# Loading each expert's up matrix in two halves, and waiting for each half in the up pass

## The reference

```python
aff = sigmoid(xt @ w_router)                      # 64 experts, 8 of them per token
...
def expert_block(args):
    rows, e = args
    xb = x_pad[rows]
    h = jax.nn.silu(xb @ w_gate[e]) * (xb @ w_up[e])
    return h @ w_down[e]
...
return (routed + shared).reshape(B, S, D)         # routed: gated sum over the chosen experts
```

## Time and profile before

| | before |
|---|---|
| median of 3 runs | 1285.56 us (1285.19 to 1286.29) |
| the profiled execution's own time | 1285.14 us |
| its span, first to last instruction | 1282.9 us |
| TensorE matmul busy | 1215.6 us (95%) |
| VectorE / ScalarE busy | 366.9 us (29%) / 293.0 us (23%) |
| moved by DMA | 446.60 MB in 70800 packets, mean 348 GB/s |
| queue of SP, share of the 16 engines over the span | 83.9% |

### The profile page before, as it was taken

The page is one execution under the profiler, slowest core; times in us unless marked ns, Lnnn a source line. Parts: engine busy times, 40 slices in busy tenths (PEclk is TensorE's granted clock), DMA queues, the critical chain, the costliest instruction groups (busy, mean ns, idle before and its releaser), DMA issues.

```text
span 1282.9 us, 20916 instructions
## 1 busy us (share of the span) xinstructions
PE 1215.6 (95%) x7984; PEld 768.6 (60%) x7986; DVE 366.9 (29%) x913; ACT 293.0 (23%) x703; POOL 49.8 (4%) x97
## 2 busy tenths in 40 slices
PE   7999999999999999999899989999999999999994
PEld 6775756565565656565677647565656655565652
DVE  0334712221222222221424447222212222222214
ACT  1453312121221212121123313121212212121211
POOL 1331000000000000000012100000000000000000
PEclk9999999999999999999999989999999999999998
DMA  9532499999999999999930525999999999999993
GB/s 345 189 138 122 202 398 421 420 421 423 422 421 422 422 422 421 422 422 421 406 129 1 202 90 214 399 420 421 421 421 421 422 422 421 422 422 422 422 420 130
DMA packets 70800, 446.60 MB, mean 348 GB/s; under 512 B 6880, under 2 KB 10336, under 8 KB 20576
## 3 DMA queue, kind: packets, MB, share of 16 engines
q1 hardware_dynamic: 69744, 442.79, 83.9%
q10 hardware_dynamic: 1008, 3.15, 0.6%
HBM read 444.86 MB, written 1.05 MB: 348 GB/s over the span
## 4 chain that ended last, share of the span: by engine, by line
issue 49%; PE 36%; DMA 10%; DVE 1%; POOL 1%; ACT 1%; SPq 0%; another core or an unknown queue 0%; POOLq 0%; DVEq 0%; ACTq 0%
DMA ring<-in_w_up 10%; PE bank L953 7%; PE bank L978 6%; PE bank L946 6%; PE bank L524 4%; PE bank L987 3%; PE bank L582 3%; PE bank L543 2%; POOL soft L501 1%; PE bank L846 1%; DMA ring<-in_w_in_a 1%; PE bank L960 1%; PE bank L758 1%; PE bank L864 1%; PE bank L558 1%
## 5 line engine op out<-in xcount | busy, mean ns | idle before, releaser
L953 PE MATMUL bank<-ring,work 128*64 128x256 f32 x2048 | 232.9, 380 | 21.3 <-DMA ring<-in_w_up 21.3
L978 PE MATMUL bank<-ring,work 128*64 128x512 f32 x1024 | 233.8, 598 | 4.3 <-ACT work L1057 4.3
L946 PE MATMUL bank<-ring,work 128*64 128x256 f32 x2048 | 232.4, 379 | 2.3 <-DMA ring<-in_w_gate 1.3
L946 PEld LDWEIGHTS bank<-ring,work 128*64 128x64 f32 x2048 | 150.9, 137 | 100.4 <-issue 39.8
L953 PEld LDWEIGHTS bank<-ring,work 128*64 128x64 f32 x2048 | 154.4, 137 | 91.9 <-issue 29.0
L1554 DVE TENSOR_TENSOR yhalf<-bank,yhalf 128x512 fp32r<-128x512 f32 x128 | 88.6, 692 | 239.4 <-ACT yhalf L1057 239.4
L987 PE MATMUL bank<-yhalf,back 128*128 128x512 f32 x512 | 150.8, 417 | 2.8 <-DVE yhalf L1554 2.8
L978 PEld LDWEIGHTS bank<-ring,work 128*64 128x64 f32 x1024 | 68.1, 136 | 134.3 <-issue 128.4
L1546 DVE SCALAR_TENSOR_TENSOR work<-work,gcol,bank 128x256 f32<-128x256 f32 x64 | 30.8, 481 | 370.2 <-issue 289.7
L1057 ACT ACTIVATE yhalf<-bank 128x512 fp32r<-128x512 f32 x128 | 76.5, 598 | 220.5 <-PE bank L978 220.5
L987 PEld LDWEIGHTS bank<-yhalf,back 128*128 128x128 f32 x512 | 87.3, 190 | 39.7 <-issue 23.8
(11 more groups left out here) (149 smaller groups left out, 754.5 us busy)
## 6 DMA issues: line engine op xcount, KB each, us to landing
ring<-in_w_gate SPq DMA_DIRECT2D x128, 1024.0 KB, 19.5
ring<-in_w_up SPq DMA_DIRECT2D x128, 1024.0 KB, 21.2
ring<-in_w_down SPq DMA_DIRECT2D x128, 1024.0 KB, 18.9
ring<-in_w_in_b SPq DMA_DIRECT2D x3, 3072.0 KB, 23.4
ring<-in_w_out SPq DMA_DIRECT2D x4, 2048.0 KB, 8.2
ring<-in_w_mem_kv SPq DMA_DIRECT2D x2, 2048.0 KB, 18.6
ring<-in_w_in_a SPq DMA_DIRECT2D x1, 3072.0 KB, 17.4
ring<-in_w_shared_gate SPq DMA_DIRECT2D x2, 1024.0 KB, 6.0
```

The costliest lines, as they stand in the source:

```text
L946: last = pe.matmul(gate_bank[slots_of(e), 0:HID], xg[:, k, slots_of(2 * j + e)], w[e][:, k, 0, :], start=(k == 0), stop=(k == KT - 1))
L953: last = pe.matmul(up_bank[slots_of(e), 0:HID], xg[:, k, slots_of(2 * j + e)], w[e][:, k, 1, :], start=(k == 0), stop=(k == KT - 1))
L978: last = pe.matmul(yb[half][slots_of(e), :], hT[:, f, slots_of(e)], w[e][:, f, half * 512:half * 512 + 512], start=(f == 0), stop=(f == FT ...
```

## The change

Each expert now has four parts instead of three: gate, first half of up (row blocks 0 to 3), second half of up (row blocks 4 to 7), down. Each half has a semaphore of its own (`up_first_landed`, `up_second_landed`). In `reload` both experts' first halves are issued ahead of both second halves. In the up pass PE waits for both first halves ahead of k = 0, and for both second halves ahead of k = 4. The bytes moved are the same, and so is the arithmetic.

```diff
-                dst, src = expert_loads(ring[:, slot, :], *srcs)[part]
-                sp.dma_start(dst, src).then_inc(sem(("gate_landed", "up_landed", "down_landed")[part] + f"{k}_{l}"), 16)
+                gate_up_down = expert_loads(ring[:, slot, :], *srcs)
+                if part in (1, 2):
+                    dst, src = gate_up_down[1]
+                    rows = slice((part - 1) * KT // 2, part * KT // 2)
+                    sp.dma_start(dst[:, rows, :], src[:, rows, :]).then_inc(sem(("up_first_landed", "up_second_landed")[part - 1] + f"{k}_{l}"), 16)
+                else:
+                    dst, src = gate_up_down[2 * part // 3]
+                    sp.dma_start(dst, src).then_inc(sem(("gate_landed" if part == 0 else "down_landed") + f"{k}_{l}"), 16)
...
                 sp.wait_ge(sem(f"hidden_{l}"), units)
-                for k in (2 * b, 2 * b + 1):
-                    expert(l, i, k, 1)
+                for part in (1, 2):
+                    for k in (2 * b, 2 * b + 1):
+                        expert(l, i, k, part)
...
-                    for e in range(2):
-                        pe.wait_ge(s_(f"up_landed{2 * b + e}"), rs * 16 + 16)
                     for k in range(KT):
+                        for e in range(2):
+                            if k == 0:
+                                pe.wait_ge(s_(f"up_first_landed{2 * b + e}"), rs * 16 + 16)
+                            elif k == KT // 2:
+                                pe.wait_ge(s_(f"up_second_landed{2 * b + e}"), rs * 16 + 16)
                         for e in range(2):
                             last = pe.matmul(up_bank[slots_of(e), 0:HID], xg[:, k, slots_of(2 * j + e)], w[e][:, k, 1, :],
                                              start=(k == 0), stop=(k == KT - 1))
```

More of the change, by code:

```diff
@@ L382, in reload @@
                 sp.wait_ge(sem(f"hidden_{l}"), units)
-                for k in (2 * b, 2 * b + 1):
-                    expert(l, i, k, 1)
+                for part in (1, 2):
+                    for k in (2 * b, 2 * b + 1):
+                        expert(l, i, k, part)
                 sp.wait_ge(sem(f"down_done_{l}"), 2 * units)
                 for k in (2 * b, 2 * b + 1):
-                    expert(l, i, k, 2)
+                    expert(l, i, k, 3)
             rows = [(lamrow[:], lambda_qk[0].rearrange("(o a) b -> o a b", o=1).broadcast_to([P, 4, HD])),
@@ L410, in _ @@
                     used(sp, last_in[l, (expert_slot0[l] + k) % RING])
-                    for part in range(3):
+                    for part in range(4):
                         expert(l, 0, k, part)
```

## The result

| | before | changed |
|---|---|---|
| median of 6 runs | 1285.38 us | 1297.82 us (1294.89 to 1298.89) |
| ratio, 95% interval | 1 | 1.0093 (1.0082 to 1.0104) |
| profiled execution, own time and span | 1285.14, 1282.9 us | 1298.89, 1296.7 us |

The changed kernel is slower by 12.0 us by the ratio (10.5 to 13.4), where 9.5 were forecast. Its profiled execution is the slowest of its six runs, so it shows a little more than the ratio does. Every ratio compares only the runs within 1.5% of a kernel's fastest, which matters for experiment 2 alone: there these are two of eight (1916.69 and 1930.34 us), while its median of 1967.03 us is that of all eight.

What follows compares the result with a forecast made beforehand. The prediction took the never-empty DMA stream as the bound of the expert stages: 1285.14 + 9.5 for smaller packets + 0 for three other terms = 1294.6 us, median 1295.0, range 1288.5 to 1299.

Steps and rivals of the forecast that it cites:

- the likeliest case: Whole kernel: DMA stream longer by 6 to 11 us, so 1291 to 1297 us; chance 0.80.
- The bound: Both layers' expert stages: DMA bounds from first reload to last landing, 14.91 us per unit against PE's 14.09.
- The smaller packets: Up reloads in both streams: 4 KB packets instead of 8 KB and one more closing packet add 9.5 us.
- The closing packet: Ends each transfer on each engine: 8.6 ns, one more per split up load.
- the 79 ns per load: Added time per up reload and engine: 8 x 8.8 ns for packets plus 8.6 ns; 120 reloads give 9.5 us.
- Octet, rate, packets: Expert stages: late four-unit period 60.3 us, rate from 422 to about 417 GB/s, packets from 200 to 400 us up 32%.
- The last down passes: Stream ends: layer 0's starts 4 to 5 us later than 616.41, layer 1's 9 to 10 us later than 1260.90.
- The waits: PE in the expert stages: the up pass's waits become more and shorter, with about as much idle time in all.
- The end of the stream: Layer 0's last down pass starts 1.0 us earlier at best, given back waiting for w_in_b; bounds -1.1 and 0, taken 0.
- Free packets: Rival, DMA stream: engines hide packet overhead, 422 GB/s stays, 1285.1 us, at best 1.1 less; chance 0.07.
- PE's waits as the price: Rival, late expert stage: PE's chain sets the pace and halving removes 18 waits, 21.3 us, giving 1263.8; chance 0.05.
- a queue held up by each transfer's closing: Rival, DMA queue: 2.3 us per added transfer, 1561 us in all, or 1309 for a twentieth; chance in part 0.06.
- A stall of PE in the middle of the pass: Rival, up pass: 1.3 us per unit makes PE the bound at 15.4 us against DMA's 15.1, 1346 us; chance 0.02.

Runs made afterwards that it cites:

- experiment 2: Against the kernel before: each up matrix in two transfers of 64 partitions x 8 KB, all waited for ahead of the up pass; 1967.03 us, ratio 1.4966.
- experiment 6: Kernel before with only row blocks 0 to 3 in the up pass, all loads as they were; 1285.25 us, ratio 1.0004.
- experiment 1: Changed kernel's half loads, but PE waits for all four halves ahead of the up pass; 1295.98 us, ratio 1.0085 to the kernel before.
- experiment 3: Changed kernel, but one reload transfer carries the same up half of both experts: 4 KB pieces, as many transfers as before; 1296.04 us, ratio 1.0081.
- experiment 7: Changed kernel with ScalarE's load of layer 1's norm rows issued some 30 us later; 1293.9 us, ratio 1.0070 to the kernel before.
- experiment 8: Kernel before with the load of layer 1's norm rows issued later; 1284.05 us, ratio 0.9992.
- experiment 11: Kernel before with each pair's two gate, two up and two down matrices in one 2 MB transfer each in the reloads, 8 KB packets; 1286.1 us, ratio 1.0014.
- experiment 5: Against the kernel before: gate, up and down matrices all in two transfers of 4 KB packets, waited for ahead of each pass; 1313.17 us, ratio 1.0226.
- experiment 10: Changed kernel with all four halves waited for ahead of the up pass and layer 1's norm rows loaded late; 1292.74 us, ratio 1.0072 to the kernel before.

## Why the prediction was right, and where it was off

**The forecast and its range.** The median of 1297.82 us is inside the range of 1288.5 to 1299, by 1.2 us, but above the 1291 to 1297 that the likeliest case was given; a second measurement gave 1296.08. The mechanism held, and what the forecast lacks is one term, below.

**The bound: right.** DMA sets the expert stages (experiment 6), so 1.8 us per unit of earlier PE work bought nothing.

**The smaller packets: right in size.** Forecast were 9.5 us on the two streams; the traces have 9.7, 9.4, 10.4 and 9.3 (changed kernel twice, experiments 1 and 3), and 9.6 where nothing else differs (experiments 7 and 8). The price held for all three matrices (28.4 forecast, 29.1 measured). Measured in the stream itself, 200 to 400 us of the changed kernel, a 4 KB piece takes (3200 - 6763 x 0.3102 - 1694 x 0.0086) / 6814 us = 159.6 ns, where the forecast had 159.5. So close an agreement is partly luck. The two small loads behind the 159.5 send one 4 KB row to every partition, which isn't how the halves are read, and their figure is a sum of records, set against an elapsed time for the 8 KB pieces; like against like the forecast's working gave 5.1 ns per pair of pieces and 5.9 us. (Its upper bound comes to 10.1 ns per packet and 10.7 us, not 10.2 and 10.8.) The split between the packets did not hold as well. The closing packet was given 8.6 ns, but taking away half of all closing packets (experiment 11) moved no more bytes, so it costs less than its record, or nothing, and the 79 ns per load are nearly all in the eight added pieces.

**Octet, rate, packets: right.** 60.24 us for 60.3, 417 to 418 GB/s for 417, 32% more packets for 32%. The last down passes were to start 4 to 5 and 9 to 10 us later; they started 5.3 and 13.8 us later in the first trace and 4.8 and 10.6 in the second.

**The waits: wrong in their place.** "The up pass's waits should become more and shorter" failed: they vanished. The "about as much PE idle time in all" failed too: 33.2 us of waits for expert weights instead of 22.6. An estimate from the rows says why. Where PE waits for gate, gate's landing sets when it starts; at 418 GB/s the first halves of up are through 2.5 us later and the second halves 5.0 us later, while the gate pass takes 3.5 us and with half the up pass 5.3. So the halves of up are there in time, and PE's waits fall on gate and down. In experiment 1, where all of up is waited for ahead of the pass, they are back at up.

**The end of the stream: the term that was mis-sized.** It was "Bounds of this term: -1.1 and 0. I take 0", on the ground that an earlier down pass is given back at the wait for w_in_b. The down pass is earlier and that is given back, but more than that is lost: PE waits longer there (1.77 and 2.33 us instead of 1.14), and in some executions the clock is then at its lower level, which costs 1.7 us more. PE comes earlier against the stream because it now starts the last down pass at the landing of its matrix, for which it waits 0.61 us, where before it started some 1.0 us after it by the forecast's own working. The wait itself comes with the norm rows, which ScalarE loads beside the last piece of w_in_b: with these later it is gone in both kernels. Between the layers the two traces of the changed kernel have +0.9 and +2.7 us, outside the term's bounds. With the streams' 9.4 and 9.7 us and the 0.3 and 1.3 us ahead of the first reload, that is the measured 10.7 and 13.8 us of span. With the wait gone in both kernels (experiments 7 and 8) the term is -0.2 us.

**The rivals.** Free packets are refuted by experiment 5, PE's waits as the price by experiment 6, and a queue held up by each transfer's closing by experiments 3 and 11. A stall of PE in the middle of the pass at its forecast size (1346 us) is refuted by the result itself; experiments 1 and 10 show no smaller one.

## What to carry to other kernels

Where the DMA engines are full and the bandwidth is flat, as in this kernel's expert stages, finer waits for loads buy nothing, and pieces half as long cost: price a split by the number of added pieces (some 10 ns of an engine each here, at 2 and at 4 KB), or look for the elapsed time of pieces of that size elsewhere in the trace. An engine off the bound that gets faster comes early to the next wait; look at what it waits for there, and at the clock behind it. Where a load has to be split, split it along the row run: the split by partitions cost 50% here.

## What was unexpected of the hardware

- With a third of the bytes in transfers of 64 partitions, the whole stream went at about half the rate with all engines full: 225 GB/s and 583 ns for the mean 8 KB packet, against 422 GB/s and 310 ns with 128 partitions (experiment 2). The Trainium skill ("DMA: Bandwidth & Descriptors", "The descriptor swizzle") says of a transfer to 128 partitions that half of the engines write partitions 0 to 63, through the even-numbered of 16 ports, and the other half partitions 64 to 127, through the odd ones, and that on this chip transfers issued by SP or ScalarE are split over the engines the same way as those issued by GpSimd. Engines that all write to half the ports at once could slow the up transfers, but the up transfers at half the rate account for 19.9 of the 28.0 us per unit only. No run here separates the ports from another cause.
- After waits of 2.26, 2.33, 3.07 and 3.12 us at the same place PE's clock was at its lower level, and after waits of 0.88 to 1.77 us it was not, all ahead of the same 32 matmuls. The length of the wait does not settle it everywhere: at the start of the kernel the 32 matmuls on w_in_a took 7.29 us behind waits of 1.93 and 1.95 us, and 10.13 us behind one of 1.94.
- SP's own issues stretch: four up issues took 4.48 us in the changed kernel, two took 0.81 to 1.47 us before at the same stage. With the engines 101.6% full the stream shows no loss by it. That it is the full queue which holds SP back is likely but not shown.
